# A state-space scan stage: input and gate products in split passes, the numbers prepared beside the norm, rotation tables on two engines

## Time and profile before

| | |
|---|---|
| median of three runs | 4040.86 us (4040.41 to 4052.23) |
| profiled execution, its time | 4044.16 us |
| profiled execution, its span | 4042.5 us |
| PE matmul, busy | 3721.5 us (92%) |
| PE weight load, busy | 2965.1 us (73%) |
| DVE, busy | 1703.9 us (42%) |
| ACT, busy | 1277.1 us (32%) |
| POOL, busy | 301.0 us (7%) |
| granted PE clock, mean | 0.961 of full speed |

### The profile page before, as it was taken

One profiled execution on the slowest core, in us unless ns is written; L12 is line 12 of the kernel. 1 busy time (PEld: TensorE's weight loads), 2 busy tenths in 40 slices (PEclk: granted clock), 3 DMA queues, 4 the chain that ended last, 5 costly groups with the idle time before them and its releaser, 6 DMA issues. The chain is left out here.

```text
span 4042.5 us, 51723 instructions
## 1 busy us (share of the span) xinstructions
PE 3721.5 (92%) x20512; PEld 2965.1 (73%) x20512; DVE 1703.9 (42%) x2607; ACT 1277.1 (32%) x1796; POOL 301.0 (7%) x247
## 2 busy tenths in 40 slices
PE   8999798799999998768889999999889899899997
PEld 7999676699999997435555888888634377447886
DVE  4442377344334432253333443443258633225432
ACT  4331466233223321123332432342110143104321
POOL 0000222000000000010000000000045232000000
PEclk9999899799999999879999999999989999999999
DMA  4322311022222223000002222222212231223221
GB/s 166 131 77 79 112 53 48 32 94 88 80 99 89 90 79 126 8 21 16 1 1 94 93 94 93 104 93 88 99 39 78 89 96 53 101 75 114 94 85 71
DMA packets 115307, 318.04 MB, mean 79 GB/s; under 512 B 13335, under 2 KB 56471, under 8 KB 99060
## 3 DMA queue, kind: packets, MB, share of 16 engines
q1 hardware_dynamic: 115188, 316.48, 22.8%
HBM read 307.95 MB, written 17.01 MB: 80 GB/s over the span
## 5 line engine op out<-in xcount | busy, mean ns | idle before, releaser
L326 PE MATMUL acc<-fb_xh,fb_wh 128*128 128x264 f32 x1408 | 287.9, 286 | 11.7 <-DVE fb_wl L476 11.7
L326 PE MATMUL acc<-fb_xl,fb_wh 128*128 128x264 f32 x1408 | 288.3, 286 | 0.0
L326 PE MATMUL acc<-fb_xh,fb_wl 128*128 128x264 f32 x1408 | 287.7, 286 | 0.0
L326 PE MATMUL acc<-fd_xh,fd_wh 128*128 128x512 f32 x704 | 275.4, 391 | 9.6 <-DVE fd_wl L476 9.6
L326 PE MATMUL acc<-fd_xl,fd_wh 128*128 128x512 f32 x704 | 274.4, 390 | 0.0
L326 PE MATMUL acc<-fd_xh,fd_wl 128*128 128x512 f32 x704 | 274.4, 390 | 0.0
L326 PEld LDWEIGHTS acc<-fb_xh,fb_wh 128*128 128x128 f32 x1408 | 220.1, 189 | 12.1 <-DVE fb_wl L476 11.9
L326 PEld LDWEIGHTS acc<-fb_xl,fb_wh 128*128 128x128 f32 x1408 | 219.4, 189 | 0.0
L326 PEld LDWEIGHTS acc<-fb_xh,fb_wl 128*128 128x128 f32 x1408 | 219.1, 189 | 0.0
L397 ACT ACTIVATE fb_wh<-fb_raw 128x2048 fp32r<-128x2048 f32 (+1 forms) x74 | 124.7, 1685 | 290.1 <-PE acc L385 177.0
L471 DVE TENSOR_TENSOR fb_wl<-fb_raw,fb_wh 128x2048 fp32r<-128x2048 f32 (+1 forms) x74 | 148.3, 2004 | 141.4 <-ACT fb_wh L397 140.5
(11 more groups left out here) (523 smaller groups left out, 8472.2 us busy)
## 6 DMA issues: line engine op xcount, KB each, us to landing
fb_raw<-wi_dram SPq DMA_DIRECT2D x42, 1024.0 KB, 4.7
fd_raw<-wi_dram SPq DMA_DIRECT2D x42, 1024.0 KB, 4.7
fb_raw<-wo_dram SPq DMA_DIRECT2D x32, 704.0 KB, 3.9
fd_raw<-wo_dram SPq DMA_DIRECT2D x32, 704.0 KB, 4.0
fa_raw<-wi_dram SPq DMA_DIRECT2D x20, 1024.0 KB, 4.7
ff_raw<-wi_dram SPq DMA_DIRECT2D x20, 1024.0 KB, 4.7
a_raw<-a_qkv_dram SPq DMA_DIRECT2D x24, 512.0 KB, 4.0
s_gw<-gate_w_dram SPq DMA_DIRECT2D x24, 512.0 KB, 3.9
```

Source lines behind the costliest of these rows:

```text
L326: last = pe.matmul(acc[:, up_base(p, b) + 2 * a + q, 0:w], x[:, k, a, :], part[:, k, t0:t0 + w], start=k == 0 and part is xh and x is wv, ...
```

## The change

- u and the gates are computed in split form, as the heads stage did it: `product` issues 24 fp32r passes for a chunk instead of 8 full-fp32 matmuls. All 28 weight chunks (4 for u, 24 for the gates) pass through a ring of four buffers: ACT rounds (`round_weights`), POOL subtracts (`rest_of_weights`), PE multiplies. x is rounded by ACT, and its rest formed by POOL (`rest_of_x`), as the norm delivers it; `xh` and `xl` stay for the heads stage, which no longer forms them.
- The normed x is written to two buffers only, each freed by POOL's rest. The squares of the norm are all ACT's. DVE computes dt and the angles ahead of the reciprocal.
- SP issues the small constants ahead of the weights, and stores a gate six chunks behind its load.
- `c_wide` moves from DVE to POOL. The doubling of `fine` moves from POOL to DVE, ahead of the b weights.
- EARLY is 2 instead of 3, so that 22 gates lie in the loop; steps 0, 2, 5, 8, 10 and 13 have two. In POOL's stream, the rests of a step's gates (for the chunk two gates later) stand behind that step's turn. In ACT's stream, the rounding for the chunk two gates later stands ahead of each sigmoid.

```diff
@@ -1736,14 +1739,18 @@
...
-            EARLY = 3
+            EARLY = 2
+            CH, RING, NU = KC * P, 4, 4
+            CHUNKS = NU + GATES
...
-            c_t = sb(st, "s_c_t", [P, 2, SC, P])
+            c_t = room[:, :, :].rearrange("p k t -> p (k t)").rearrange("p (r s c) -> p r s c", r=2, s=SC)
             d = sb(st, "s_dt", [P, 4])
-            gw = sb(st, "s_gw", [P, 3, KC * P])
+            raw = sb(st, "s_raw", [P, RING, CH])
+            wh = sb(st, "s_wh", [P, RING, CH], F32R)
+            wl = sb(st, "s_wl", [P, RING, CH], F32R)
+            turns = sb(st, "s_turns", [P, 3, 2, SEQ])
             gates = sb(st, "s_gates", [P, GATES_HELD, SEQ])
-            w = sb(st, "s_w", [P, 4, KC * P])
...
+            xn = turns[:, 0, :, :]
+            fine_t = work[:, 8, 0:SC * FINE // 2]
...
+                    def weights(j):
+                        sp.dma_start(raw[:, j % RING, :], s_u[j] if j < NU else gate_w[j - NU]
+                                     ).then_inc(there[j % RING], 16)
...
-                    sp.dma_start(w[:, :, :], s_u.rearrange("c p n -> p c n")).then_inc(u_there, 16)
                     sp.dma_start(a[:, :, :], s_a).then_inc(c_in, 16)
                     sp.dma_start(b_in_[:, :, :, :], s_b).then_inc(c_in, 16)
                     sp.dma_start(c_in_[:, :, :, :], s_c).then_inc(c_in, 16)
                     sp.dma_start(d[:, :], s_d).then_inc(c_in, 16)
-                    for n in range(GATES):
-                        if n >= 3:
-                            sp.wait_ge(gate_mm, 1 + n - 2)
-                        sp.dma_start(gw[:, n % 3, :], gate_w[n]).then_inc(gate_there[n % 3], 16)
-                        if n >= 3:
-                            store_gate(sp, n - 3)
-                    for n in range(GATES - 3, GATES):
-                        store_gate(sp, n)
+                    for j in range(RING):
+                        weights(j)
+                    STORED_AFTER = NU + 6
+                    for j in range(RING, CHUNKS):
+                        sp.wait_ge(split, 1 + j - RING + 1)
+                        weights(j)
+                        if j >= STORED_AFTER:
+                            store_gate(j - STORED_AFTER)
+                    for n in range(CHUNKS - STORED_AFTER, GATES):
+                        store_gate(n)
...
@@ -1806,8 +1819,33 @@
                                        pattern=[[16, 8]], channel_multiplier=-1).then_inc(shape, 1)
                     for table in (fine, coarse):
                         pool.memset(table[:, 0, :, 0:1], 1.0)
-                        pool.memset(table[:, 1, :, 0:1], 0.0)
+                        last = pool.memset(table[:, 1, :, 0:1], 0.0)
+                    last.then_inc(zeroed, 1)
+                    pool.wait_ge(c_in, 65)
+                    pool.wait_ge(shape, 4)
+                    pool.tensor_scalar(c_in_[:, 1, :, :], c_in_[:, 1, :, :], -1.0, None, ALU.mult)
                     pool.drain()
+                    for n in range(8):
+                        last = pool.tensor_scalar(c_wide[:, :, :, n * 64:(n + 1) * 64].rearrange("p r c s -> p (r c) s"),
+                                                  c_in_[:, :, :, :].rearrange("p r c s -> p (r c) s"),
+                                                  groups[:, n:n + 1], None, ALU.mult)
+                    last.then_inc(c_wid, 1)
+
+                    def rest_of_weights(j):
+                        pool.wait_ge(rounded, 1 + j + 1)
+                        pool.tensor_tensor(wl[:, j % RING, :], raw[:, j % RING, :],
+                                           wh[:, j % RING, :].bitcast(F32), ALU.subtract).then_inc(split, 1)
+
+                    def rest_of_x(k):
+                        pool.wait_ge(x_hi, 1 + k + 1)
+                        pool.tensor_tensor(xl[:, k, :], xn[:, k % 2, :], xh[:, k, :].bitcast(F32),
+                                           ALU.subtract).then_inc(x_lo, 1)
+
+                    rest_of_weights(0)
+                    for k in range(KC):
+                        rest_of_x(k)
+                    for j in range(1, RING):
+                        rest_of_weights(j)
 
                     def double(table, k, n):
 
...
                             double(coarse, k, (1 << k) // FINE)
-                    pool.wait_ge(u_mm, 5)
+                    for j in range(RING + EARLY, RING + 2 * EARLY):
+                        rest_of_weights(j)
+                    pool.wait_ge(fined, 2)
                     t = spare[:, :].rearrange("p (a b) -> p a b", a=COARSE)
                     for s in range(SC):
                         if s >= 3:
@@ -1850,30 +1890,35 @@
                                 pool.drain()
                         last.then_inc(spun, 1)
                         pool.drain()
+                        for n in at_step[s]:
+                            if NU + n + 2 < CHUNKS:
+                                rest_of_weights(NU + n + 2)
 
                 @block.tensor
                 def _(pe):
...
-                            if c == 0:
-                                pe.wait_ge(normed, 1 + k + 1)
-                            last = pe.matmul(acc[:, c, :], w[:, c, k * P:(k + 1) * P], xn[:, k, :],
-                                             start=k == 0, stop=k == KC - 1)
-                        last.then_inc(u_mm, 1)
+                    for c in range(NU):
+                        product(c, acc[:, c, :]).then_inc(u_mm, 1)
 
                     def gate(n):
-                        pe.wait_ge(gate_there[n % 3], 1 + 16 * (n // 3 + 1))
                         if n >= 2:
                             pe.wait_ge(gated, 1 + n - 1)
-                        for k in range(KC):
-                            last = pe.matmul(acc[:, GATE_BANK[n % 2], :], gw[:, n % 3, k * P:(k + 1) * P], xn[:, k, :],
-                                             start=k == 0, stop=k == KC - 1)
-                        last.then_inc(gate_mm, 1)
+                        product(NU + n, acc[:, GATE_BANK[n % 2], :]).then_inc(gate_mm, 1)
 
                     for n in range(EARLY):
                         gate(n)
@@ -1924,21 +1969,37 @@
 
                 @block.scalar
                 def _(act):
-                    for c in range(0, KC, 2):
+                    def round_weights(j):
+                        act.wait_ge(there[j % RING], 1 + 16 * (j // RING + 1))
+                        act.activation(wh[:, j % RING, :], raw[:, j % RING, :], ACT.Copy).then_inc(rounded, 1)
+
+                    for c in range(KC):
                         if c >= 2:
                             act.wait_ge(summed, 1 + c - 1)
-                        act.activation(nsq[:, 0, :], h[:, c, META:], ACT.Square).then_inc(sq_a, 1)
+                        act.activation(nsq[:, c % 2, :], h[:, c, META:], ACT.Square).then_inc(sq_a, 1)
+                    round_weights(0)
                     act.wait_ge(summed, 1 + KC)
                     act.activation(rstd[:, :], acc[:, 4, :], ACT.Sqrt, scale=1.0 / D, bias=eps_t[:, :]
                                    ).then_inc(rooted, 1)
-                    for c in range(4):
+                    for k in range(KC):
+                        act.wait_ge(normed, 1 + k + 1)
+                        act.activation(xh[:, k, :], xn[:, k % 2, :], ACT.Copy).then_inc(x_hi, 1)
+                    for j in range(1, RING):
+                        round_weights(j)
+                    for c in range(NU):
                         act.wait_ge(u_mm, 1 + c + 1)
+                        if c < EARLY:
+                            round_weights(c + RING)
                         act.activation(u[:, c, :], acc[:, c, :], ACT.Copy).then_inc(u_ready, 1)
                     act.wait_ge(ang, 2)
                     act.activation(v[:, SIN, :], v[:, ANG, :], ACT.Sin)
                     act.activation(v[:, HALF, :], v[:, ANG, :], ACT.Sin, scale=0.5).then_inc(sins, 1)
 
                     def gate(n):
+                        if NU + n + 2 < CHUNKS:
+                            if n >= 2:
+                                act.wait_ge(gate_mm, 1 + n - 1)
+                            round_weights(NU + n + 2)
                         act.wait_ge(gate_mm, 1 + n + 1)
                         if n >= GATES_HELD:
                             act.wait_ge(gates_stored[n % GATES_HELD], 16 * (n // GATES_HELD))
...
                     dve.wait_ge(c_in, 65)
-                    dve.wait_ge(shape, 4)
...
+                    dve.wait_ge(rooted, 2)
+                    dve.reciprocal(rstd[:, :], rstd[:, :])
+                    dve.drain()
+                    for c in range(KC):
+                        if c >= 2:
+                            dve.wait_ge(x_lo, 1 + c - 1)
+                        dve.scalar_tensor_tensor(xn[:, c % 2, :], h[:, c, META:], gain[:, 7, c:c + 1], rstd[:, :],
+                                                 ALU.mult, ALU.mult).then_inc(normed, 1)
                     exact_exp(MAG, Z)
```

(42 more changed lines are left out.)

84 lines of the change are left out of this document (34 added, 50 removed).

## The result

The changed kernel takes 4108.94 us (median of four runs, 4102.53 to 4113.52). The kernel before, timed beside it, takes 4043.28 us. The ratio is 1.0154, 95% interval 1.0141 to 1.0166: by the ratio slower by 62 us (57 to 67). The forecast was 4077 us, slower by 36, with a range of 4056 to 4104. So the sign was right and the size was too small: the time is 32 us above the forecast and 5 us above the range, the slowdown by the ratio 26 us larger than forecast.

What follows compares the result with a forecast made beforehand. PE was taken to set the scan loop of the kernel before. Loop +32, tail -4 and head +8 make +36 us on 4044.2, so 4080, and 4077 us with the median 3.3 lower; range 4056 to 4104.

Steps and rivals of the forecast that it cites:

- Split products: Scan stage: 28 split products save PE 42 us; by busy time the loop shrinks from 204.3 to about 180 us.
- The new waits in the loop: Scan loop: late POOL turns make six of fifteen steps take 20.6 us instead of 10.73 (the first 19); +32 us.
- Rival 3: Scan loop: PE idles about 7 us after each late turn and its clock makes it worse; over +63 us, chance 0.05.
- The tail: End of the scan loop: the last result starts 13.1 us after step 15's start instead of 17.3; -4 us.
- The head: Scan stage up to DVE's first step: -4 us by its steps, +8 us with POOL and DVE blocking each other.
- (a): Head, DVE's angles beside the norm: ready in 8.3 us, normed x +2 us; blocking by POOL taken as 8 us.
- (b): Head, normed x passing DVE, ACT and POOL: POOL's pace of 8 x 1.35 us, plus 4 us of blocking.
- (d): Head, fine table on DVE: 30 operations taken as 8.5 us, with bounds of 5 and 20 us.
- (e): Head, b weights 6.6 us, then their transposes and the first inputs about 9 us, no longer hidden beneath POOL.
- The heads stage: Stage behind the scan: loses eight ACT copies and eight DVE subtractions, first product still waits; 0, at most -1 us.
- Rivals 1 and 2: Loop: turns not late, faster (chance 0.10); stalls half as many or long, +8 to +20 us (within 12 us: 0.07).
- rival 1: Scan loop: turns not late, PE or DVE bounds it; loop 180 us instead of 204.3, whole -16 to -28; chance 0.10.

Runs made afterwards that it cites:

- e3: Against the changed kernel, 26 matmuls with unused results fill PE's idle time in each of six steps; 4087.9 us, ratio 1.0106 to the kernel before.
- e4: Against the changed kernel, DVE computes the b weights ahead of the fine table's doublings; 4082.8 us, ratio 1.0092 to the kernel before.
- e1: Against the changed kernel, POOL runs turn s+1 ahead of the rests of step s; 4043.4 us, ratio 0.9997 to the kernel before.
- e2: Against the changed kernel, ACT rounds each gate's weight chunk behind the sigmoid two gates earlier; 4047.5 us, ratio 1.0003 to the kernel before.

## Why the prediction fell short

*Split products.* Right. A pass starts 0.233 us after the one before (0.227 forecast), and once the queues are repaired the loop takes 179 to 182 us, where "about 180" was given. The gain in the loop was there and the order took it.

*The new waits in the loop.* The mechanism, its place and the count of six were right: the rests wait for ACT's roundings, the turns stand behind them. The term that was mis-sized is the 20.6 us of a cycle, and in it the pieces "3.7 (y and inputs) + 5.4 (gate)", both taken at full clock. Measured were 24.7 us on average for the five later cycles. Fifteen steps took 238.8 us instead of 219.3: that is 19.5 of the missing 26 us. e3 shows that 20.8 is what the cycle costs when PE is kept busy, so the sum was whole and only the clock was wrong. The first cycle took 17.7 us where the forecast had 19 "but a low clock"; PE was at full clock there (granted 1.00 from 3026 to 3040, its passes 0.233 us apart), so the low clock was put where it was not and left out where it was.

*Rival 3* named the cause, but I gave it as a tail (0.05 for over +63). No run shows the +27 us by which the high end stands above the forecast: it was my estimate. What the runs showed in its place is a granted clock of 0.50 from 3053 to 3065 behind 6.8 us of idle and of 0.95 from 3065 to 3069, five later cycles of 24.7 us on average, and a loop 18.6 us shorter once the idle places are filled (e3). The earlier trace rows already showed the clock at 0.52 some 10 us after an idle of 11 us. The idle ahead of each cycle, 6.8 us, came out of my own sum, so a low clock behind it belonged in the likeliest case. The low end of the range (+17) does not follow from the terms either: +36 without the 12 us of mutual blocking is +24. It played no part, since the time lies beyond the high end.

*The tail.* -4.7 us against -4: right.

*The head.* +14.4 us against +8, which is the rest of the missing 26. Step by step:
- (a), c_wide and the rest of chunk 0 beside the numbers, was put at +8 and cost 4.5 (the numbers took 12.8 us instead of 8.3). POOL's pieces took 1.55 us each, not 1.05, and still blocked less. Several of DVE's operations seem to pass between two POOL instructions; that reading was not tested by itself.
- (b), x in turns, was right: 3.79 us for two chunks where POOL's own pace was put at 2 x 1.35, +4 us over eight.
- (d), the fine table, was 10.1 us against 8.5, inside its bounds.
- (e), the b weights, is the step that failed: "6.6 us" was 15.1. I took the row of before, where POOL ran short doublings beside it, and did not ask what POOL would run there after the change: two rests of 2.4 us and turn 0. In e4, beside short doublings, the same operations take 7.0 us. I had looked for the mutual blocking at the two places where the change puts work on POOL, and not where it moves DVE's work beside POOL's.

The cost of the blocking to DVE was measured: in the changed kernel two of its 128x16 operations, of 0.17 us when undisturbed, last 2.11 and 2.31 us beside two rests on POOL (4.66 together), and in e1 a copy lasts 1.33 us beside a turn instead of 0.42.

*The heads stage*, 0 to -1: right within 1 us.

Rivals 1 and 2 fell; rival 1's loop of 180 us is what the kernel has once the order is mended.

## What to carry to other kernels

In a queue that runs strictly in order, ask of each added wait what stands behind it and for which engine that is urgent; here moving one loop line (e1), or rounding two gates earlier (e2), was worth 70 us of loop. When a forecast contains a new idle of PE, price what PE does next at the low clock too (0.50 behind each idle of 6.8 us here). When work on DVE moves, look at what POOL runs beside its new place, and at which work was hidden beneath something else before and is not any more.

## What the runs showed of the hardware

- PE's granted clock was 0.50 of full speed behind each idle of 6.8 us in the loop. It stayed there for 3.3 to 4.0 us of its work or for about 12, with the same code (changed kernel and e4). Filled with useless matmuls, the same places kept 1.00 (e3).
- An eighth of c_wide (128x512, one scalar a partition) took 1.55 us on POOL (all eight within 1.56 to 1.61, beside DVE's small operations) and 0.41 on DVE, where each of the first two operations of a turn on POOL, of the same size and with two operands, takes 1.05.
- Beside POOL's long instructions (a rest is 2.34 to 2.42 us) DVE's short ones took up to 2.2 us longer each. POOL lost less: the first two pieces of a turn took 1.22 to 1.28 us instead of 1.05 beside DVE's wide operations in e1. Of two DVE operations without a drain between them the second did not wait in the changed kernel (2.11, then 0.16; 2.31, then 0.16), while in e4 both did (2.23, then 2.40, of 0.23 undisturbed). In the loop DVE's multiplications, additions and subtractions (128x512, one operand in PSUM) took 0.68 to 0.70 us beside turns and rests.
